# A step list on VectorE, handed out by TensorE's count: no steps inside a norm, no debt carried over it, and a smaller weight for one step

## The reference, cut to what matters

```python
q = (xt @ wq).reshape(t, PEER_HEADS, 2, HALF_Q)
scores = jnp.einsum('thpd,hpnd->thpn', q, keys)
s_top, i_top = lax.top_k(scores, PEER_TOPK)
...
u = jnp.take(u_tab, eb, axis=0)
a = jax.nn.gelu(jnp.einsum('td,thkd->thk', xb, u), approximate=False)
w = (gb * a)
vv = jnp.take(v_tab, eb, axis=0)
return jnp.einsum('thk,thkd->td', w, vv)
```

## Time and profile before

| | us |
|---|---|
| median of 3 runs (2775.79 to 2789.11) | 2776.78 |
| the profiled execution | 2782.02 |
| its span | 2780.2 |
| TensorE busy in it | 2247.7 |
| VectorE busy in it | 1614.7 |
| GpSimd busy in it | 958.3 |

### The profile page before, as it was taken

How to read it: one execution, slowest core, us unless ns; L and a number is a source line. 1 busy time by engine, 2 the same in 40 slices (tenths; PEclk the granted TensorE clock), 3 DMA queues, 4 the chain that set the end, 5 groups by cost and what they waited for, 6 DMA issues and landing times.

```text
span 2780.2 us, 24763 instructions
## 1 busy us (share of the span) xinstructions
PE 2247.7 (81%) x8716; PEld 1576.3 (57%) x8716; DVE 1614.7 (58%) x3608; ACT 630.5 (23%) x1698; POOL 958.3 (34%) x772
## 2 busy tenths in 40 slices
PE   7999989989888987987787888778333589999990
PEld 6877768647667765666466536647322444444440
DVE  0023212113448567897665666866988777766667
ACT  2233122122112213231211103011687520000000
POOL 0000000000014333443554564633577235565555
PEclk9979999989999958998888998888555699999995
DMA  5523334434258866775889898966679369999997
GB/s 157 156 76 99 114 118 154 156 130 136 94 201 303 260 204 223 269 274 211 310 315 337 298 399 305 355 227 219 198 261 343 105 223 349 335 410 409 409 408 281
DMA packets 317168, 683.53 MB, mean 246 GB/s; under 512 B 21234, under 2 KB 175090, under 8 KB 316788
## 3 DMA queue, kind: packets, MB, share of 16 engines
q0 software_dynamic: 110592, 402.70, 39.5%
q1 hardware_dynamic: 200384, 266.54, 28.3%
q10 hardware_dynamic: 6068, 12.71, 1.3%
HBM read 679.78 MB, written 2.10 MB: 245 GB/s over the span
## 4 chain that ended last, share of the span: by engine, by line
PE 47%; DVE 21%; DMA 13%; POOL 8%; issue 6%; ACT 5%; ACTq 0%; another core or an unknown queue 0%; DVEq 0%; POOLq 0%
PE bank L608 46%; POOL SLOT L2213 8%; DVE SLOT L1672 7%; DMA SLOT<-in_peer_u,EI 7%; DMA SLOT<-in_peer_v,EI 5%; DVE ACC L1686 1%; ACT SPREAD L2137 1%; DVE X L1686 1%; DVE PB L1244 1%; PE bank L633 1%; DVE OH L1577 1%; DVE OH L1581 1%; DVE EX L1584 1%; ACT XS L1752 1%; PE bank L756 1%
## 5 line engine op out<-in xcount | busy, mean ns | idle before, releaser
L2213 POOL DMA_INDIRECT SLOT<-in_peer_u,EI x512 | 654.8, 1279 | 1521.6 <-DVE T L1536 880.5
L608 PE MATMUL bank<-HT,W 128*128 128x256 f32 x4032 | 949.7, 398 | 77.2 <-issue 51.3
L608 PEld LDWEIGHTS bank<-HT,W 128*128 128x128 f32 x4032 | 799.2, 200 | 207.9 <-issue 65.9
L1672 DVE CUSTOM_DVE_ANT_0 SLOT<-SLOT,H 128x1024 f32<-128x1024 f32 x384 | 454.8, 1222 | 47.9 <-DMA SLOT<-in_peer_u,EI 45.1
L2213 POOL DMA_INDIRECT SLOT<-in_peer_v,EI x256 | 303.3, 1185 | 278.0 <-DVE ACC L1686 138.9
L608 PE MATMUL bank<-H,SPREAD 128*128 128x512 f32 x680 | 305.9, 598 | 8.6 <-DMA H<-in_peer_v 8.1
L608 PEld LDWEIGHTS bank<-H,SPREAD 128*128 128x128 f32 x680 | 125.0, 190 | 182.8 <-issue 132.3
L1686 DVE SCALAR_TENSOR_TENSOR X<-SLOT,AA,X 128x1024 f32<-128x1024 f32 x128 | 164.5, 1285 | 70.0 <-DMA SLOT<-in_peer_v,EI 66.3
L1672 DVE CUSTOM_DVE_ANT_0 SLOT<-SLOT,ACC 128x1024 f32<-128x1024 f32 x128 | 153.8, 1223 | 76.3 <-DMA SLOT<-in_peer_u,EI 76.2
L1686 DVE SCALAR_TENSOR_TENSOR ACC<-SLOT,AA,ACC 128x1024 f32<-128x1024 f32 x128 | 164.1, 1282 | 10.0 <-DMA SLOT<-in_peer_v,EI 0.9
L608 PE MATMUL bank<-JK,SPREAD 128*128 128x512 f32 x344 | 156.1, 596 | 2.1 <-DMA JK<-in_peer_v 2.1
(11 more groups left out here) (297 smaller groups left out, 2421.1 us busy)
## 6 DMA issues: line engine op xcount, KB each, us to landing
W<-in_w_in SPq DMA_DIRECT2D x68, 1024.0 KB
W<-in_w_up SPq DMA_DIRECT2D x44, 1024.0 KB
H<-in_peer_v SPq DMA_DIRECT2D x85, 512.0 KB
JK<-in_peer_v SPq DMA_DIRECT2D x43, 512.0 KB
W<-in_w_down SPq DMA_DIRECT2D x20, 1024.0 KB
W<-in_peer_wq SPq DMA_DIRECT2D x16, 1024.0 KB
W<-in_w_o SPq DMA_DIRECT2D x8, 1024.0 KB
W<-in_w_out SPq DMA_DIRECT2D x8, 1024.0 KB
```

What stands on the lines that cost most here:

```text
L608: return e.matmul(out, lhsT, rhs, start=start, stop=stop)
L1672: e.tensor_tensor_reduce(out=x, in0=x, in1=NORMED[t], scale=1.0, scalar=0.0, op0=ALU.mult, op1=ALU.add, accum_out=AA[t % 2][:, k:k + 1]).t ...
L2213: e.indirect_dma_start(out=SLOT_OF[s], out_offset=None, in_=a["peer_v_2"] if i >= P else a["peer_u_2"], in_offset=bass.IndirectOffsetOnAxi ...
```

## The change

The weight of a job in the count becomes 1.6 instead of 1.8 at all places. Inside `norm` nothing is handed out, the flat addition of 4 per tile is gone, and behind a norm the count is cut to at most 2.0.

```diff
-HEAD = 9.0
+HEAD, JOB = 9.0, 1.6
...
-    jobs = [[("job", t, which * P + k, 1.8) for k in range(P)] for t, which in ROWS_OF[g]]
+    jobs = [[("job", t, which * P + k, JOB) for k in range(P)] for t, which in ROWS_OF[g]]
...
-            state = {"bank": 0, "tile": 0, "spent": 0.0, "side": None, "at": 0, "until": 0}
+            state = {"bank": 0, "tile": 0, "spent": 0.0, "side": None, "at": 0, "until": 0, "quiet": False}
...
-                tick()
+                if not state["quiet"]:
+                    tick()
...
             def norm(g, name):
+
                 pace("norm", g, name)
+                state["quiet"] = True
                 for t in range(GB):
-                    state["spent"] += 4
                     for half in range(2):
...
                         k.then_inc(*p_norm.mark("tr", g, name, t, half))
+                state["quiet"], state["spent"] = False, min(state["spent"], 2.0)
```

More of the change, by code:

```diff
@@ L1069, in tensor @@
                 if g:
-                    settle(("job", GB * (g - 1), 2 * P - 1, 1.8), "queries", g)
+                    settle(("job", GB * (g - 1), 2 * P - 1, JOB), "queries", g)
                 queries(g)
@@ L1073, in tensor @@
                     state["side"], state["at"], state["spent"] = g, LEAD[g], 0.0
-                    state["until"] = EXPERTS[g].index(("job", GB * g, 2 * P - 1, 1.8))
+                    state["until"] = EXPERTS[g].index(("job", GB * g, 2 * P - 1, JOB))
             spread()
```

## The result

The change made the kernel slower: 2796.42 us, the median of 11 runs, against 2775.49 for the kernel before, measured beside it (11 runs). The ratio is 1.0071, with a 95% interval of 1.0050 to 1.0092: about 20 us. The direction and the range of the prediction hold; the predicted 2788 is 8 us low. By the prediction's own division (above 2790.7) this is "slower", to which it had given 0.40, a little less than to "same" (0.42).

A forecast was written before the change was run, and what follows sets the result against it. It took VectorE to bound the attention, late weights the MLP features, full DMA the second part. Norms give back 16 us, the moved jobs cost 27: +11.1 from the median 2776.8 gives 2788 us, range 2764 to 2807.

The forecast's parts named there:

- Norms: Pair 1's norms without steps: g2 -9.8 us, gf2 -4.0, g1 -2.3, gm2 0.
- the mixer's tail: Sign of being right: pair 1's tail of the mixer, 27.7 us before, becomes about 24 us.
- the five pauses: Sign of being right: TensorE's five pauses in the MLP features, about 43 us before, sum to 45 to 52 us.
- the wait for ATB: Sign of being right: TensorE's wait for ATB in the mixer, 13.46 us before, becomes about 18 us.
- Attention and its settled point: One more job behind the compressed keys' copies, +1.2 us; 12 more jobs on VectorE in the attention, +9 (+3 to +15).
- MLP features: 96 steps instead of 84 beside the feature products, twelve more gathers, short pauses grow: +5 us (0 to 16).
- rival D: Norm g2: VectorE comes late, the wait only moves, at most 9.8 us lost; +21, 2798 us; chance 0.10.
- Second part: MLP second part: 47 steps instead of 42 where DMA is full, +8 us (3 to 10).
- Mixer: Three more jobs up to head 0's key matmuls +4.8 us, tail -3.5; together +4 (-2 to +8).
- A (full price): Attention, features and second part pay every job, +15, +16, +10; sum +30, 2807 us; chance 0.17.
- B: Transfers are clear after the norm, MLP pauses do not grow, five sum under 40 us; -14.5, 2762 us; chance 0.15.
- C: DMA engines serve the queues in turn, so more jobs lengthen no pause, features 0; +6, 2783 us; chance 0.13.

The follow-up runs named there:

- g1 paced: The changed kernel with norm g1 given back the pace it had before, other norms quiet, weight 1.6: 2788.16 us, ratio 1.0027.
- half the bytes: The changed kernel with pair 0's gathers fetching 512 of 1024 columns of each row, VectorE at full width: one run, 2724.7 us.
- half of VectorE's work: The changed kernel with VectorE's two instructions of a job on 512 of 1024 columns, gathers untouched: one run, 2695.12 us.
- s4: The changed kernel, quiet norms, a weight per stage (projection 1.0, merge 1.2, features 1.9, second part 2.1, row products 0.8, among others): 2758.95 us, ratio 0.9939.
- the weight alone: The kernel before with a job weighing 1.6 instead of 1.8, the norms keeping their pace: 2784.32 us, ratio 1.0021.
- quiet alone: The changed kernel with the weight left at 1.8, so only the norms are quiet: 2785.65 us, ratio 1.0029.
- second profile of before: The kernel before, no edit, profiled again: 1089.8 us from norm gf2 to norm gf2, 4.0 less than in the first profile.
- MLP at 1.8: The changed kernel with weight 1.8 from norm g2's end to the second part's end, 1.6 elsewhere: 2768.45 us, ratio 0.9958.

## Why the prediction was right or wrong

- **Norms: right, to a tenth.** Forecast -9.8, -4.0, -2.3 and 0; measured -9.9, -4.0 and -2.3, with norm gm2's own time unchanged. Of the signs that I had named, the two norms, the wait ahead of gm2 and the mixer's tail (26.7 to 23.5 us) came as said, the five pauses (52.6, said 45 to 52) and the wait for ATB (19.20, said 18) a little higher.
- **Attention and its settled point: the sum right by luck, the split wrong.** Forecast +1.2 and +9; measured +8.8 (477.7 to 486.5), of which 3.9 ahead of the first PCT and 4.9 behind it. I had put the 9 to twelve more jobs on a full VectorE. They cost 4.1 to 5.0 in the four kernels with weight 1.6 there. The other part is what a quiet g1 leaves for the settled point: 4.9 against the run with g1 paced, and 9.5 at weight 1.8, which I had priced at 1.2. Together with it norm g1's gain of 2.3 is a loss. The two errors cancel.
- **MLP features: the term that was mis-sized.** Forecast +5 (0 to 16); measured +9.9 against one profile of before and +14.0 against the other. The bound was right: half the bytes take the pauses away, half of VectorE's work does not. What sets the size is open. Among the kernels with quiet norms the three with 92 jobs of full bytes take 219.4 to 222.6 us and the six with 82 take 199.1 to 213.4, but s4 takes 221.6 with 78, and the weight alone 208.2 with 92. A candidate for the last are the gathers that a quiet norm does not start, as stretches of norm g2 show. The changed kernel:

```profile
1358.00:1368.00 10.00, 5.47 (x22) 4.42 (x23) 5.13 (x5) 4.19 (x11) 2.19 (x2) 0.64 0.47 150
```

The weight alone:

```profile
1365.00:1375.00 10.00, 0.00 (x0) 0.00 (x0) 8.39 (x9) 0.00 (x0) 6.94 (x7) 0.50 0.98 386
```

  TensorE waited in the paced norm, but the DMA engines worked (386 GB/s); in the quiet one they move 150. Norm and features together take 230.8 us with the weight alone and 232.7 in the changed kernel: at this weight the whole gain of norm g2 came back as pauses. That is the outcome of rival D by another road: I had looked whether VectorE came late into the norm, and not at what its transfers were worth. At weight 1.8 the same two stages fall from 232.7 and 228.6 to 217.5 and 222.1, so there the quiet norm does gain. That speaks against the candidate: quiet alone moves only 128 GB/s in its norm g2 and has short features, s4 moves 339 and has long ones. It is not shown.
- **Second part: right.** Forecast +8 for five more jobs, measured +9.7, near the upper end. The step of one rate per job (1.89 us) holds only from some 42 steps on.
- **Mixer: a little small.** Forecast +4.8 to ATB and +4 in all; measured +6.2 and +7.0. The activation at L2158 cost more than the 1.5 taken: the wait for KET is 6.36, and the gain in the tail (3.2, forecast 3.5) pays only for a part of it. I had let VectorE wait for ScalarE there. It is ScalarE that waits, 11.58 us for VectorE's last job, and holds back KET. With half of VectorE's work per job the wait for KET is 0.24 us.
- **Rivals.** A (full price) has the second part right (+10), the features a little high (+16) and the attention too high (+15). B's condition, pauses under 40 us, came true only with 81 or 82 jobs in the features (39.2 in the second profile of before, 39.3, 36.8 and 30.7). On C: the longest pauses are 11.23 before, 13.08 after, and 11.70 and 12.10 in two kernels with other counts; a full pause hardly grows with more jobs, what changes is how many of them are full, and by s4 the number of jobs alone does not decide that. The page "DMA: Bandwidth & Descriptors" of the Trainium skill, section "Queues, rings and completion order", has the engines take packets from the queues with work in turn. The packet counts of the second part are near to that (6865 and 7072), those of the pause less so (776 and 1124). Such turns would give a ceiling to a pause. But the gathers' packets are larger, so the weights had only a third of the time in both places. From the turns alone I had the features pay nothing, and they paid: the short pauses filled up.

In the sum: forecast +11.1, in the two first profiles +19.2 up to the queries, and +19.7 by the ratio. Most of the 8 us missing are the features (4.9) and the mixer (3.0). That 19.2 and 19.7 agree is in part luck, since the whole spans of these two profiles differ by 14.0 and those of the changed kernel and the second profile of before by 21.8. The last stretch, for which I had no term, differs by -8.0 and -3.9; of that, 4.1 is the spread of one program.

## What to carry to other kernels

A step list that is handed out by a count has to be judged as a whole: a pause in it, even where it frees the engine that waits, can be paid at the next fixed point, as behind norm g1 and in the queries here. There the postponed steps arrive as one burst, and the gathers of its last ones come late. Give each stage its own weight by the resource that is short in it, and set the weights so that no fixed point finds a backlog. Before silencing a stage in which the bounding engine idles, look at which other resource works in that time, here DMA at 386 GB/s; whether that work is missed later was not shown here. Two profiles of the old kernel tell how far a stage bound by transfers can be sized at all.

## What the runs showed of the hardware

- With the DMA engines full, the queue with the larger packets had two thirds of their time: 6865 packets of gathers (3.6 KB) take 68.1% in the second part and 7072 of weights (1.7 KB) 34.2%; in a pause of the features it is 776 (3.7 KB, 72.1%) and 1124 (1.0 KB, 32.4%).
- With rows of 2 KB instead of 4 KB the second part's share and rate fell from 1.02 and 393 GB/s to 0.85 and 286: 385 GB/s for a full engine set became 336. The smaller rows alone are not shown as the cause, since the weights' queue, whose transfers are the same, fell as much: from 367 to 336 GB/s of its own time, the gathers' from 392 to 337.
- Two profiles of one program agree to 0.5 us in every stage but the MLP features and the last stretch, where they differ by 4.1 us each. The second part, which transfers fill, agrees to 0.3.
- A pause costs TensorE a little more than itself. With the weight alone the granted clock is 0.50, the lower of its two levels (1.2 GHz), in a 10 us stretch in which TensorE does nothing. The 128 products behind a pause of 10 us or more take 30.1 to 30.9 us in the changed kernel, and 28.4 (a quarter of 113.42) where there are no pauses and the mean clock is 0.98. A short pause can cost as much behind it as a long one: behind the pauses of 3.21 and 3.24 us in the kernel with the MLP at 1.8 they take 30.75 and 30.82. In the 5.7 us behind the first of these the granted clock is 0.50, and from 1410 to 1430 it is 1.00.
